# A modulation GEMV moved from GpSimd to VectorE in a two-block transformer kernel

## The reference

```
c_act = jax.nn.silu(c)                          # [1, 2048]
mod = c_act @ w_mod[l] + b_mod[l]               # l = 0, 1: w_mod [2, 2048, 6144]
mod = c_act @ w_mod_kv + b_mod_kv               # w_mod_kv [2048, 4096]
shift, scale, gate = jnp.split(mod, 3, axis=-1)
h = x * (1.0 + scale[:, None]) + shift[:, None]
x = layer_norm(alpha * x + gate[:, None] * y, ln_g[l], ln_b[l])
```

## Time and profile before

| | |
|---|---|
| median of three runs | 2972.42 us |
| span of the profiled execution | 2965.1 us, 7.3 us less than the median |
| busy: TensorE, VectorE, ScalarE, GpSimd | 2702.1, 1774.0, 1222.6, 1637.6 us |
| last GEMV load issued | 2081.6 us |
| moved by DMA | 604.67 MB, mean 204 GB/s |

### The profile page before, as it was taken

The page is one execution under the profiler, slowest core; times in us unless marked ns, Lnnn a source line. Parts: engine busy times, 40 slices in busy tenths (PEclk is TensorE's granted clock), DMA queues, the critical chain, the costliest instruction groups (busy, mean ns, idle before and its releaser), DMA issues.

```text
span 2965.1 us, 37109 instructions
## 1 busy us (share of the span) xinstructions
PE 2702.1 (91%) x12005; PEld 2128.3 (72%) x12005; DVE 1774.0 (60%) x1786; ACT 1222.6 (41%) x1575; POOL 1637.6 (55%) x1060
## 2 busy tenths in 40 slices
PE   7987999998899888888888999998999879999987
PEld 6765787876677666666666777766788768888876
DVE  5789867757455555455545666655457556545645
ACT  4354333335333433333333333333458444444643
POOL 6986777774038999999989877798200000000000
PEclk9999999999999999999999999999999989999999
DMA  7776676776466777777676767766654536565453
GB/s 228 221 227 215 204 236 198 212 226 226 152 189 216 223 226 224 223 223 222 219 224 224 241 224 244 226 225 223 210 163 145 177 109 207 181 210 172 125 184 132
DMA packets 312714, 604.67 MB, mean 204 GB/s; under 512 B 26590, under 2 KB 28644, under 8 KB 310668
## 3 DMA queue, kind: packets, MB, share of 16 engines
q1 hardware_dynamic: 301628, 571.92, 61.5%
q10 hardware_dynamic: 10960, 31.10, 2.8%
HBM read 592.31 MB, written 10.62 MB: 203 GB/s over the span
## 4 chain that ended last, share of the span: by engine, by line
PE 42%; POOL 36%; issue 9%; DVE 8%; DMA 2%; ACT 2%; POOLq 1%; SPq 1%; DVEq 0%; ACTq 0%
POOL gemv_w L497 19%; POOL gemv_acc L507 14%; PE bank L566 12%; PE bank L568 11%; PE bank L567 11%; DVE w_lo L1649 3%; PE bank L654 2%; POOL gemv_acc L495 1%; PE bank L530 1%; POOL gemv_lo L511 1%; DVE sq L1795 1%; POOL gemv_hi L505 1%; DMA gemv_w<-in_kv_w_mod 1%; DMA raw<-in_w_ffn_down 1%; ACT w_hi L1067 1%
## 5 line engine op out<-in xcount | busy, mean ns | idle before, releaser
L1649 DVE TENSOR_TENSOR w_lo<-raw,w_hi 128x1024 fp32r<-128x1024 f32 x820 | 1252.2, 1532 | 1087.1 <-ACT w_hi L1067 1069.1
L1067 ACT CAST w_hi<-raw 128x1024 fp32r<-128x1024 f32 x820 | 860.1, 1050 | 1593.3 <-PE bank L568 815.1
L497 POOL TENSOR_TENSOR gemv_w<-gemv_w,small 128x512 f32<-128x512 f32 x480 | 735.9, 1533 | 183.8 <-DMA gemv_w<-in_w_mod 161.2
L507 POOL TENSOR_TENSOR gemv_acc<-gemv_acc,gemv_w 128x512 f32<-128x512 f32 x480 | 766.3, 1596 | 72.5 <-POOL gemv_w L497 68.9
L566 PE MATMUL bank<-w_hi,u_hi 128*128 128x512 f32 x1408 | 586.2, 416 | 93.2 <-DVE w_lo L1649 86.5
L568 PE MATMUL bank<-w_hi,u_lo 128*128 128x512 f32 x1408 | 564.2, 401 | 0.0
L567 PE MATMUL bank<-w_lo,u_hi 128*128 128x512 f32 x1408 | 563.7, 400 | 0.0
L566 PE MATMUL bank<-w_hi,s_hi 128*128 128x512 f32 x1280 | 520.8, 407 | 19.8 <-DVE w_lo L1649 16.6
L568 PE MATMUL bank<-w_hi,s_lo 128*128 128x512 f32 x1280 | 509.4, 398 | 0.0
L567 PE MATMUL bank<-w_lo,s_hi 128*128 128x512 f32 x1280 | 509.1, 398 | 0.0
L566 PEld LDWEIGHTS bank<-w_hi,u_hi 128*128 128x128 f32 x1408 | 269.4, 191 | 207.4 <-DVE w_lo L1649 138.7
(11 more groups left out here) (337 smaller groups left out, 2289.2 us busy)
## 6 DMA issues: line engine op xcount, KB each, us to landing
gemv_w<-in_w_mod SPq DMA_DIRECT2D x384, 256.0 KB, 3.0
raw<-in_w_in SPq DMA_DIRECT2D x176, 512.0 KB, 4.1
raw<-in_a_w_in SPq DMA_DIRECT2D x128, 512.0 KB, 3.9
raw<-in_w_ffn_gate SPq DMA_DIRECT2D x88, 512.0 KB, 4.3
raw<-in_w_ffn_up SPq DMA_DIRECT2D x88, 512.0 KB, 3.8
raw<-in_w_ffn_down SPq DMA_DIRECT2D x88, 512.0 KB, 4.2
gemv_w<-in_kv_w_mod SPq DMA_DIRECT2D x128, 256.0 KB, 3.0
raw<-in_kv_w SPq DMA_DIRECT2D x64, 512.0 KB, 3.7
```

What stands on the lines that cost most here:

```text
L497: pool.tensor_tensor(gemv_w[:, k % 2], gemv_w[:, k % 2], c_k, ALU.mult).then_inc(gemv_scaled, 1)
L507: ins = pool.tensor_tensor(gemv_acc[:], gemv_acc[:], gemv_w[:, k % 2], ALU.add)
L1067: act.copy(w_hi[:, s], raw[:, s]).then_inc(hi_done, 1)
L1649: dve.tensor_tensor(w_lo[:, s], raw[:, s], w_hi[:, s].bitcast(F32), ALU.subtract).then_inc(lo_done, 1)
```

## The change

The GpSimd program goes. VectorE does each GEMV step in its iteration j, behind the split of that iteration: a `tensor_scalar` for the first step of a chunk, one fused `scalar_tensor_tensor` (multiply, add) for each other, two of them at the last, and the subtraction for `gemv_lo`. In the SP queue the load of step j no longer follows the load of unit j but that of unit j+2 (GEMV_LAG = 2); the last two steps of a body are loaded in the first two places of the next body, so the loops have their first bodies written out. The waits of the loads keep their counts. Where `finish` runs, the step stands ahead of it.

```diff
+        GEMV_LAG = 2
@@ SyncE @@
-            def wide_body(pr, i, w, col, mod_w=None, mod_col=None):
+            def tail_of(pr, gemv):
+                def issue(j):
+                    gemv(pr.units - GEMV_LAG + j)
+                return issue
+            def gemv_behind(j, gemv, tail):
+                if j >= GEMV_LAG:
+                    gemv(j - GEMV_LAG)
+                elif tail:
+                    tail(j)
+            def wide_body(pr, i, w, col, gemv, tail):
                 half = pr.units // 2
                 for j in range(pr.units):
                     load(pr, i, j, w, j % half, col + (j // half) * COLS)
-                    load_gemv(pr, i, j, mod_w, mod_col)
+                    gemv_behind(j, gemv, tail)
...
@@ GpSimd: the whole program @@
-                for k in range(KD):
-                    pool.wait_ge(gemv_landed[k % 2], i * (8 * KD) + 16 * (k // 2 + 1))
-                    c_k = c_act[:, k:k + 1].broadcast_to([P, COLS])
...
-                        pool.tensor_tensor(gemv_w[:, k % 2], gemv_w[:, k % 2], c_k, ALU.mult).then_inc(gemv_scaled, 1)
-                        pool.wait_ge(gemv_scaled, i * (KD - 1) + k)
-                        pool.wait_ge(gemv_step, i * KD + k)
...
-                        ins = pool.tensor_tensor(gemv_acc[:], gemv_acc[:], gemv_w[:, k % 2], ALU.add)
-                    ins.then_inc(gemv_step, 1)
...
@@ VectorE @@
+            def gemv(pr, i, j):
+                if not pr.mods:
+                    return
+                part = pr.units // pr.mods
+                m, k = j // part, j % part
+                if k >= KD:
+                    return
+                n = pr.mod0 + m
+                c_k, w_k = c_act[:, k:k + 1], gemv_w[:, k % 2]
+                dve.wait_ge(gemv_landed[k % 2], i * (pr.mods * 8 * KD) + (n * 8 * KD + 16 * (k // 2 + 1)))
+                if k == 0:
...
+                    dve.tensor_scalar(gemv_acc[:], w_k, c_k, None, ALU.mult).then_inc(gemv_step, 1)
+                    return
+                dve.wait_ge(gemv_step, i * (pr.mods * KD) + (n * KD + k))
+                if k == KD - 1:
...
+                    dve.scalar_tensor_tensor(out=gemv_hi[:], in0=w_k, scalar=c_k, in1=gemv_acc[:], op0=ALU.mult,
+                                             op1=ALU.add).then_inc(gemv_cut, 1)
+                dve.scalar_tensor_tensor(out=gemv_acc[:], in0=w_k, scalar=c_k, in1=gemv_acc[:], op0=ALU.mult,
+                                         op1=ALU.add).then_inc(gemv_step, 1)
+                if k == KD - 1:
...
+                    dve.tensor_tensor(gemv_lo[:], gemv_acc[:], gemv_hi[:].bitcast(F32), ALU.subtract).then_inc(gemv_cut, 1)
...
-                    if finish and j == pr.units - 2:
+                    ending = finish and j == pr.units - 2
+                    if ending:
+                        gemv(pr, i, j)
                         finish()
                     if not isinstance(i, int) or pr.unit0 + i * pr.units + RING + j < limit:
                         split(pr, i, j)
+                    if not ending:
+                        gemv(pr, i, j)
```

More of the change, by code:

```diff
@@ L327, in block_kernel @@
         gemv_landed = (sem("gemv_landed0"), sem("gemv_landed1"))
-        gemv_scaled, gemv_cut = sem("gemv_scaled"), sem("gemv_cut")
+        gemv_cut = sem("gemv_cut")
         gemv_step, mod_sum, mod_copied, mod_stored = sem("gemv_step"), sem("mod_sum"), sem("mod_copied"), sem("mod_stored")
@@ L433, in load_gemv, with gemv_of, issue @@
                 sp.dma_start(gemv_w[:, k % 2], w[k * P:(k + 1) * P, ds(col + m * COLS, COLS)]).then_inc(gemv_landed[k % 2], 16)
-            def wide_body(pr, i, w, col, mod_w=None, mod_col=None):
+            def gemv_of(pr, i, mod_w, mod_col):
+                def issue(j):
+                    load_gemv(pr, i, j, mod_w, mod_col)
+                return issue
+            def tail_of(pr, gemv):
+                def issue(j):
+                    gemv(pr.units - GEMV_LAG + j)
+                return issue
+            def gemv_behind(j, gemv, tail):
[4 more added lines that the diff above has]
+            def wide_body(pr, i, w, col, gemv, tail):
                 half = pr.units // 2
@@ L439, in wide_body, with two_weights @@
                     load(pr, i, j, w, j % half, col + (j // half) * COLS)
-                    load_gemv(pr, i, j, mod_w, mod_col)
+                    gemv_behind(j, gemv, tail)
+            def two_weights(pr, i, pair, gemv, tail):
+                for j in range(pr.units):
+                    load(pr, i, j, pair[2 * j // pr.units][0], j % (pr.units // 2), i * COLS)
+                    gemv_behind(j, gemv, tail)
             pr = products["qkv"]
-            wide_body(pr, 0, w_in[0], 0, w_mod_2[0], 0)
+            gemv0 = gemv_of(pr, 0, w_mod_2[0], 0)
+            wide_body(pr, 0, w_in[0], 0, gemv0, None)
             with sp.Fori(1, pr.bodies) as i:
-                wide_body(pr, i, w_in[0], i * 2 * COLS, w_mod_2[0], i * COLS)
+                wide_body(pr, i, w_in[0], i * 2 * COLS, gemv_of(pr, i, w_mod_2[0], i * COLS),
+                          tail_of(pr, gemv_of(pr, i - 1, w_mod_2[0], (i - 1) * COLS)))
+            last = tail_of(pr, gemv_of(pr, pr.bodies - 1, w_mod_2[0], (pr.bodies - 1) * COLS))
             pr = products["spill"]
-            wide_body(pr, 0, w_in[0], 3 * W1, w_mod_2[0], pr.mod0 * COLS)
+            wide_body(pr, 0, w_in[0], 3 * W1, gemv_of(pr, 0, w_mod_2[0], pr.mod0 * COLS), last)
             with sp.Fori(1, pr.bodies) as i:
-                wide_body(pr, i, w_in[0], i * 2 * COLS + 3 * W1 + 2 * H1, w_mod_2[0], i * COLS + pr.mod0 * COLS)
+                wide_body(pr, i, w_in[0], i * 2 * COLS + 3 * W1 + 2 * H1, gemv_of(pr, i, w_mod_2[0], i * COLS + pr.mod0 * COLS),
+                          tail_of(pr, gemv_of(pr, i - 1, w_mod_2[0], (i - 1) * COLS + pr.mod0 * COLS)))
+            last = tail_of(pr, gemv_of(pr, pr.bodies - 1, w_mod_2[0], (pr.bodies - 1 + pr.mod0) * COLS))
             pr = products["branch"]
[L451 to L454, removed]
+            none = gemv_of(pr, 0, None, None)
+            two_weights(pr, 0, (w_branch_gdn, w_branch_moba), none, last)
+            with sp.Fori(1, pr.bodies) as i:
+                two_weights(pr, i, (w_branch_gdn, w_branch_moba), none, None)
+            last = None
             pr = products["w_out"]
@@ L458, in _ @@
                 layer, chunk = divmod(pr.mod0 + i, MODS[0] // COLS)
-                wide_body(pr, i, w_out[0], i * 2 * COLS, w_mod_2[layer], chunk * COLS)
+                gemv = gemv_of(pr, i, w_mod_2[layer], chunk * COLS)
+                wide_body(pr, i, w_out[0], i * 2 * COLS, gemv, last)
+                last = tail_of(pr, gemv)
             pr = products["ffn"]
[L461 to L465, removed]
+            first = pr.mod0 * COLS - MODS[0]
+            two_weights(pr, 0, (w_ffn_gate, w_ffn_up), gemv_of(pr, 0, w_mod_2[1], first), last)
+            with sp.Fori(1, pr.bodies) as i:
+                two_weights(pr, i, (w_ffn_gate, w_ffn_up), gemv_of(pr, i, w_mod_2[1], i * COLS + first),
+                            tail_of(pr, gemv_of(pr, i - 1, w_mod_2[1], (i - 1) * COLS + first)))
+            last = tail_of(pr, gemv_of(pr, pr.bodies - 1, w_mod_2[1], (pr.bodies - 1) * COLS + first))
             for name, w, col0 in (
@@ L471, in _ @@
                 pr = products[name]
-                with sp.Fori(0, pr.bodies) as i:
-                    wide_body(pr, i, w, i * 2 * COLS + col0, kv_w_mod_2,
-                              i * (pr.mods * COLS) + (pr.mod0 * COLS - MODS[0] - MODS[1]))
+                first = pr.mod0 * COLS - MODS[0] - MODS[1]
+                wide_body(pr, 0, w, col0, gemv_of(pr, 0, kv_w_mod_2, first), last)
+                with sp.Fori(1, pr.bodies) as i:
+                    wide_body(pr, i, w, i * 2 * COLS + col0, gemv_of(pr, i, kv_w_mod_2, i * (pr.mods * COLS) + first),
+                              tail_of(pr, gemv_of(pr, i - 1, kv_w_mod_2, (i - 1) * (pr.mods * COLS) + first)))
+                last = tail_of(pr, gemv_of(pr, pr.bodies - 1, kv_w_mod_2, (pr.bodies - 1) * (pr.mods * COLS) + first))
             for n in range(2 * HALVES):
@@ L1649, in split @@
                 dve.tensor_tensor(w_lo[:, s], raw[:, s], w_hi[:, s].bitcast(F32), ALU.subtract).then_inc(lo_done, 1)
+            def gemv(pr, i, j):
[9 more added lines that the diff above has]
+                if k == 0:
+                    if not (isinstance(i, int) and i * pr.mods + n == 0):
+                        dve.wait_ge(gemv_cut, i * (pr.mods * 2) + 2 * n)
+                    dve.tensor_scalar(gemv_acc[:], w_k, c_k, None, ALU.mult).then_inc(gemv_step, 1)
+                    return
+                dve.wait_ge(gemv_step, i * (pr.mods * KD) + (n * KD + k))
+                if k == KD - 1:
+                    if not (isinstance(i, int) and i * pr.mods + n == 0):
+                        dve.wait_ge(mod_stored, i * (pr.mods * 16) + 16 * n)
```

(6 more changed lines are left out.)

## The result

The changed kernel takes 5008.48 us (median of 4 runs, 5003.1 to 5018.71) against 2972.04 us for the one before on the same chip (4 runs): 1.685 times as long, interval 1.6825 to 1.6877. The span of the profiled execution is 5005.2 us, 2040.1 more than before.

What follows compares the result with a forecast made beforehand. TensorE was 91% busy, with GpSimd's GEMV setting the weight loads' pace in ffn. Span 2965 + 664 (first stretch) + 1362 (second stretch) = 4991 us, so 5000 us was predicted, range 4700 to 5350.

Steps and rivals of the forecast that it cites:

- the first stretch: Qkv and spill, up to branch's third weight load: 173 weight loads 7.7 us apart, 1332 us instead of 668, +664.
- the breaks: Four places behind down's chunks without GEMV steps: nine iterations each at TensorE's 2.81 us, 25 us each, 100 us together.
- the turns: From one GEMV step's end to the next, one weight load with whole latency: 7.7 us, bounds 7.0 to 8.25.
- the second stretch: From w_out through ffn and down to q2's fourth load: 2572 us instead of 1210, +1362.
- The circle: GEMV stretches: next weight load waits for the previous one's load, cast, split and step; 7.7 us per unit, chance 0.73.
- The other work in ffn: VectorE's work besides splits, 0.2 us per ffn iteration; covered while the weight load is under way, costed at nothing.
- The rest, 0: Branch and everything from q2 on keep their order and carry no GEMV step: change of 0.
- The third rival: In spill, delta-net hand-overs fill the cover, so VectorE's other work costs time: +269 us, 5270 us, chance 0.08.
- The lower clock of TensorE: Rival: idle TensorE drops its clock, slowing units in down's step-free places by up to 83 us, 5085 us; chance 0.09.
- The page's fit for a DMA: Weight loads: 3.2 us for 512 KB instead of 3.5 at least, giving 6.9 us per unit, near 4600 us; rejected.
- The rival in which loads keep their lead: GEMV stretches: weight loads are never held by a step and run at TensorE's pace, 2720 us; chance 0.06.

Runs made afterwards that it cites:

- the pads: One unused VectorE reduction added per step iteration to the changed kernel: between split and step 5237.76 us, at the iteration's start 5017.0 us.
- order_only: GpSimd keeps the GEMV as in the kernel before, only SP's load order changed (GEMV_LAG = 2): 2978.23 us, ratio 1.0031 to before.
- lag5: The changed kernel with GEMV_LAG = 5 instead of 2: 2785.29 us, ratio 0.9368 to the kernel before.

## Why the prediction was right

It forecast 5000 us and the kernel takes 5008. The mechanism is the one that was forecast. Its terms are off by more than the sum, and part of the closeness is luck: the first stretch cost 27 us more than forecast, the breaks 14 us more, the turns of the second stretch 26 us less.

- *The circle.* Seen in the trace as forecast, turn by turn, and shown by both swaps (step ahead of the split, lag) and by the pads.
- *The turn, 7.7 us.* The stretch in ffn gives 7.70. By terms in the turn above: 0.16 for 0.2, 0.59 for 0.55, 3.83 for 4.0, 1.08, 1.14, and 0.75 for 0.73. On the mean of ffn's 176 turns the term from the weight load to its cast is 4.00 us. The fused step is 746 ns long, 8% over the earlier trace rows. The other work in ffn, beside the circle, I divided by 188 where the earlier trace rows counts 203 splits; it is 0.2 us either way.
- *First stretch, +664.* Its step 0 ended at 42.0 and branch's third weight load went out at 1399.95, so 173 turns took 7.85 us each. Before, that load went out at 709.28 (I had read 710.5), so the difference is +691. The excess is not VectorE's other work, which I costed at nothing: in all 173 turns the cast starts within 0.12 us of the landing, and what the splits start late comes to 3 us together. The loads land later, as the lines below show for this stretch and then for ffn; the mean from load to cast is 4.12 us against 4.00. Some of these loads run beside transfers that ScalarE issues: 19 of them took 4.6 us on the mean, the other 155 took 4.0. The longest, 8.2 us, was issued at 1298.85, 3.6 us behind the 3072 KB load of `qkv_b`, which took 10.4. What delays the rest is open.

```profile
DMA to landing us min/median/max: 3.5/3.9/8.2
...
DMA to landing us min/median/max: 3.5/3.8/5.2
```

- *Second stretch, +1362.* From w_out's step 0 (its end at 1565.3) to the release at 4125.35 are 2560 us. Measured at the loads the stretch cost +1357. The nine iterations of a break took 26.4, 27.3, 26.4 and 34.3 us, 114 in all for 100; the longest holds the hand-over from down to v2. That leaves 7.62 us a turn. I named q2's fourth load as the one released last, near 2089; by the count of the queue it is the third, which before went out at 2083.68.
- *The rest, 0.* Branch -5 us, from q2 on -2.
- *The third rival's sign.* A slower pace in spill than in ffn was to mean that VectorE's other work is on the circle. The pace was slower, 7.85 against 7.70, but for the reason above, so the sign was not specific.
- *The lower clock of TensorE.* The granted clock in ffn was 0.73 on the mean [after, second stretch above] against 0.99, TensorE idle for 40% of the time. I had said that it would be some 37% busy; at the lower clock the same matmuls took longer, and it was 60% busy. But the four breaks together cost 14 us more than forecast, not 83. In the first of them TensorE was soon back at its full level, as the two stretches below (3256 to 3266 us, then 3266 to 3276) show. The rival's mechanism is real, but its price, nine units at the lower clock in each break, was too high.

```profile
3256.00:3266.00 10.00, 8.31 (x29) 6.71 (x30) 8.45 (x9) 5.37 (x6) 0.00 (x0) 0.83 0.78 248
3266.00:3276.00 10.00, 10.00 (x44) 7.79 (x43) 5.98 (x8) 3.39 (x4) 0.00 (x0) 1.00 0.46 169
```

- *The page's fit for a DMA.* The fit of the Trainium skill ("DMA: Bandwidth & Descriptors", Anatomy of one DMA, SWDGE path), which is for loads issued by GpSimd, gives 3.2 us for 512 KB as an estimate. Landings in ffn were 3.5 at least and 3.8 at the median, with the DMA engines two thirds idle; the measurement decides.
- *Chances.* The rival in which loads keep their lead had 2720 us. It is what a lag of five does, at 2785: the gain that the engine part of the change holds is real, and the order of the queue turned it into a loss. The 65 us between the two numbers are mostly the 2.81 us a unit, which ffn does not reach. That TensorE waited for splits before the change isn't in the rows that I named for it.

## What to carry to other kernels

When a step moves to another engine, redraw who waits for whom with the in-order queues in it: an instruction in front of the awaited one on its engine joins the wait, and a load behind the waiting one on SP joins it too. Count how many loads can be in flight at each place of the queue. If the release that a load waits for comes only after the load before it has landed and been used, that count is one, and every unit pays the whole latency, however deep the ring is. A lag between two interleaved streams has two ends, set by the ring of one and by the landing of the other; here two places to either side of the best lag cost 12 to 14% of the time.

## What the runs showed of the hardware

Without GpSimd's steps the split of 1024 columns takes 1.225 us everywhere (820 of them, mean 1225 ns), against 1532 ns on the mean of the whole kernel before; 1.73 in qkv and spill. With the steps back on GpSimd (order_only) it is 1525 ns again, and with a lag of five, where the DMA engines are busier than before, 1223. So GpSimd's work slows it, and not the DMAs. Another operation of two SBUF tiles, 24 times in spill, doubles its time beside GpSimd (before, then after):

```profile
L1913 DVE TENSOR_TENSOR l_level<-l_t,early 128x512 f32<-128x512 f32 x24 | 32.9, 1404 | 0.0
...
L1954 DVE TENSOR_TENSOR l_level<-l_t,early 128x512 f32<-128x512 f32 x24 | 15.6, 684 | 0.0
```

At full pace with the GEMV beside the weights (lag5 in ffn) the DMA engines are 84% busy at 269 GB/s, and weight loads land in 4.7 and 4.2 us at the median instead of 3.8 and 3.7 in the change. Nothing waits for them there:

```profile
928.00:1444.00 516.00, 512.37 (x2232) 410.58 (x2231) 373.06 (x425) 222.58 (x245) 0.00 (x0) 1.00 0.84 269
...
raw<-in_w_ffn_gate SPq DMA_DIRECT2D x88, 512.0 KB, 4.7
...
raw<-in_w_ffn_up SPq DMA_DIRECT2D x88, 512.0 KB, 4.2
```
